# First slab and input in interleaved pieces, constants later, bias rows spread by eight transfers

## The chip, the cores and the metric

The kernel runs on one core of one Trainium2 chip. The metric is the device time of one execution in microseconds (us), as the median over runs; less is better. All numbers are FP32. TensorE multiplies in the FP32R format with every operand split into a high and a low part, so that one product takes three passes.

## The reference

Two blocks of a network run one after the other on 512 tokens of width 1024. The first block has four layers. Each has a mixer (differential attention in layers 0 and 3, HGRN2 in layer 1, sliding-window attention with sinks in layer 2), a layer norm, a squared-ReLU feed-forward of width 4096, a layer norm and a gated per-layer embedding. The second block is one layer with chunkwise retention, an RG-LRU branch and a gated convolutional feed-forward. What bears on the change is the beginning, the differential attention of layer 0 with its relative bias:

```python
def diff_attention(h, w_in, lam, subln, w_out, rel_bias, layer_idx):
    q, k, v = jnp.split(h @ w_in, [DA_QK, 2 * DA_QK], axis=-1)    # 8 heads x 2 maps of 64
    ...
    for blk in range(S // BLOCK):                                   # 4 blocks of 128 queries
        s = jnp.einsum('bmqd,bmkd->bmqk', q[:, :, qs:ke], k[:, :, :ke])
        rel = pos[qs:ke, None] - pos[None, :ke]
        bias = rel_bias[t5_bucket(rel)].transpose(2, 0, 1)          # 16 bias heads
        s = jnp.where(rel >= 0, s + bias, -jnp.inf)
        a = jax.nn.softmax(s, axis=-1).reshape(B, H, 2, BLOCK, ke)
        a = a[:, :, 0] - lam_full * a[:, :, 1]
        outs.append(jnp.einsum('bhqk,bhkv->bhqv', a, v[:, :, :ke]))
```

The bias depends on the distance of query and key alone. Layer 3 uses the same bias; layer 2 uses one of its own with a window of 128.

## The kernel before, in words

**Weights** come as a stream of 287 slabs of 1 MB (128 partitions x 8 x 256), in the order in which `PLAN` lists them. SP issues one DMA a slab into a ring of three (`raw`, L371): the first three at once, slab n when the last unit of slab n - 3 is done (`unit_done`). GpSimd makes the high part of each (`high_part`, `whi`, L393), VectorE the low part (`low_parts`, `wlo`, L1393), which lies in the same bytes as `raw`. VectorE makes it at fixed places of its program, so it waits there for GpSimd, and what is behind it waits too.

**Units.** A unit is eight steps `k` over 1024 input features that fill two PSUM banks with 256 output columns: three matmuls for each of two halves (`feature_chunk`, L410 to L412) or of four token blocks (`token_chunk`, L442 to L444). `begin_unit` waits for the slab's low part (`split_done`) and for the banks of two units before.

**The opening.** ScalarE issues x in four transfers of two feature tiles (L897), then seven constants (L900: `vec`, `ident`, `swapm`, `pick`, `reset`, `tab`, `rb`; all count up the semaphore `loaded`), and makes `gh` from x; VectorE makes `gl` (L1399), with slab 0's `wlo` after the first of the four. TensorE multiplies unit 0; then `start()` multiplies the one-hot table `tab` with `rb` (L489). ScalarE copies the result to DRAM as `bias_table` [16, 1280] (16 heads, 640 values for each of two tables; L908), and when it has landed issues two transfers from DRAM to DRAM which spread the rows: `bias_da` [16, 128, 512] (L910) and `bias_sw` [16, 128, 256] (L911). In them row p of a head is the same line of the table shifted by p:

```python
act.dma_start(bias_da, bass.AP(tensor=table.tensor, offset=127, ap=[[1280, 16], [-1, P], [1, S]])).then_inc(biased, 16)
act.dma_start(bias_sw, bass.AP(tensor=table.tensor, offset=640 + 383, ap=[[1280, 16], [-1, P], [1, 256]])).then_inc(biased, 16)
```

Then ScalarE takes a few small exponentials (L914 to L919), on which a chain of small VectorE operations hangs (L1431 to L1471); behind that chain VectorE makes the low parts of slabs 2, 3 and 4.

**The mixer of layer 0** (`da_mixer`) has four groups of three units (q, k, v for two heads each). ScalarE empties the units into `da_q`, `da_k`, `da_v` (`evac`, L992 to L996). A loop over 32 iterations k (8 heads x 4 query blocks) does `scores(k)` on TensorE (L520), `mask(k)` on VectorE, which adds the bias tile `da_b` (L1591), the exponentials on ScalarE, the transposes (L533) and values (L546) of earlier iterations, and between them nine steps of the next group's units. `scores(k)` waits for `mask(k - 1)`. `bias_in(hd)` on ScalarE (L982) brings the bias of one head pair, 512 KB, from `bias_da` to one of two SBUF buffers; the first two stand between `evac(0, 1)` and `evac(0, 2)` behind a wait for both spreads:

```python
evac(0, 0)
evac(0, 1)
act.wait_ge(biased, 32)
bias_in(0)
bias_in(1)
evac(0, 2)
```

All DMAs that ScalarE issues are on one queue (q10 in the profile), all of SP's on another (q1). Both run on the core's 16 DMA engines.

Of the kernel before, what the change touches and what calls it, by code (L numbers as in the profile page):

```python
# [21 lines left out]
ALU = mybir.AluOpType  # L22
ACT = mybir.ActivationFunctionType

P = 128
S = 512
# [9 lines left out]
HEADS = 8  # L36
# [5 lines left out]
RING = 3  # L42
# [70 lines left out]
PLAN = make_plan()  # L113
N_SLABS = len(PLAN.slabs)
# [65 lines left out]
def build(nc, stream, xin, pin, pos, vecs, relb, onehot, eye, swap, picks, decay, resets, out):  # L180
    with ExitStack() as ctx:
# [11 lines left out]
        raw = place("raw", [P, RING, 8, 256])  # L193
        wlo = place("wlo", [P, RING, 8, 256], F32R, at=raw_at)
# [133 lines left out]
        def sem(name):  # L328
            return ctx.enter_context(nc.semaphore(name))
# [8 lines left out]
        act_own, dve_own = sem("act_own"), sem("dve_own")  # L338
        loaded = sem("loaded")
        x_in = [sem(f"x_in{t}") for t in range(4)]  # L340
        table_out, biased = sem("table_out"), sem("biased")
        m = {}

        def M(name):
            if name not in m:
                m[name] = sem(name)
            return m[name]
# [17 lines left out]
        @block.sync  # L365
        def _(sp):

            for n in range(N_SLABS):
                if n >= RING:
                    sp.wait_ge(unit_done, PLAN.last_unit[n - RING] + 1)  # L370
                sp.dma_start(raw[:, n % RING].rearrange("p k n -> p (k n)"), stream[n]).then_inc(raw_in[n % RING], 16)  # L371

            for t in range(KT):
                sp.wait_ge(M("final_out"), t + 1)
                sp.dma_start(out[:, t, :], fin[:, t, :]).then_inc(M("stored"), 16)
            sp.wait_ge(M("stored"), KT * 16)


        @block.gpsimd
        def _(pool):  # L380
            def low_parts(l, gen):

                for k in range(KT):
                    pool.wait_ge(M("ln_full"), 8 * l + k + 1)

                    pool.wait_ge(*((xh_ready, 4 * gen + k // 2 + 1) if k % 2 else (M("ln_h"), 4 * l + k // 2 + 1)))
                    nc.gpsimd.tensor_tensor(xl[:, k, :], h[:, k, :], xh[:, k, :].bitcast(F32), ALU.subtract)\  # L387
                        .then_inc(xl_ready if k % 2 else M("low_even"), 1)


            def high_part(n):
                pool.wait_ge(raw_in[n % RING], 16 * (n // RING + 1))
                nc.gpsimd.tensor_scalar(whi[:, n % RING], raw[:, n % RING], 1.0, 0.0, ALU.mult, ALU.add).then_inc(hi_done, 1)  # L393

            norm_at = {}
            for layer in range(NL):
                norm_at[PLAN.at[f"ffn{layer}"][0] + 2] = (2 * layer, X_GEN[f"ln1{layer}"])
                norm_at[PLAN.at[f"gate{layer}"][0] + 1] = (2 * layer + 1, X_GEN[f"ln2{layer}"])
            for n in range(N_SLABS):
                if n in norm_at:  # L400
                    low_parts(*norm_at[n])
                high_part(n)
# [3 lines left out]
        def _(pe):  # L406
# [6 lines left out]

            def begin_unit(u):

                pe.wait_ge(split_done, PLAN.unit_slab[u] + 1)
                if u >= 2:
                    e, v = PLAN.released(u - 2)
                    pe.wait_ge(rel[e], v)

            def feature_chunk(u, k, kn, w0, operand):

                slot = PLAN.unit_slab[u] % RING
                oh, ol = operand
                for j in range(2):
                    c = slice(j * P, (j + 1) * P)
                    last = passes(proj[:, 2 * (u % 2) + j, :], (whi[:, slot, w0 + k, c], wlo[:, slot, w0 + k, c]),
                                  (oh[:, k, :], ol[:, k, :]), k == 0, k == kn - 1)
                return last
# [17 lines left out]
            def operand_wait(which, gen, k):  # L447

                if k % 2 == 0:
                    hi, lo = (xh_ready, xl_ready) if which == "x" else (gh_ready, gl_ready)  # L450
                    pe.wait_ge(hi, gen * 4 + k // 2 + 1)
                    pe.wait_ge(lo, gen * 4 + k // 2 + 1)
# [42 lines left out]
            def da_mixer(d, layer):  # L495
# [3 lines left out]
                def chunk(g, c):  # L499
                    u = u0 + 3 * g + c // 8  # L500
                    k = c % 8
                    if k == 0:
                        begin_unit(u)
                    if g == 0 and c < 8:
                        operand_wait("g", gen, k)
                    last = token_chunk(u, k, 8, G) if c // 8 == 2 else feature_chunk(u, k, 8, 0, G)
                    if k == 7:
                        last.then_inc(unit_done, 1)
# [268 lines left out]
            def ret_mixer():  # L777
                s0, u0 = PLAN.at["ret"]
                gen = G_GEN["in4"]
                def chunks(u, first, end):  # L780

                    for c in range(first, end):
                        v, k = u + c // 8, c % 8
                        if k == 0:
                            begin_unit(v)
                        if v == u0:
                            operand_wait("g", gen, k)
                        last = token_chunk(v, k, 8, G) if v - u0 in (2, 3, 8, 9) else feature_chunk(v, k, 8, 0, G)
                        if k == 7:
                            last.then_inc(unit_done, 1)  # L790
# [89 lines left out]
        def _(act):  # L880
# [14 lines left out]
            for t in range(4):  # L895
                p2 = slice(2 * t, 2 * t + 2)
                act.dma_start(h[:, p2, :], xin[:, p2, :]).then_inc(x_in[t], 16)  # L897
            for dst, src in ((vec[:, :], vecs), (ident[:, :], eye), (swapm[:, :], swap), (pick[:, :, :], picks),
                             (reset[:, :], resets), (tab[:, :], onehot), (rb[0:32, :], relb)):
                act.dma_start(dst, src).then_inc(loaded, 16)  # L900
            for t in range(4):
                p2 = slice(2 * t, 2 * t + 2)
                act.wait_ge(x_in[t], 16)
# [3 lines left out]
            mine()  # L907
            act.dma_start(table, tabo[:, :]).then_inc(table_out, 16)  # L908
            act.wait_ge(table_out, 16)
            act.dma_start(bias_da, bass.AP(tensor=table.tensor, offset=127, ap=[[1280, 16], [-1, P], [1, S]])).then_inc(biased, 16)  # L910
            act.dma_start(bias_sw, bass.AP(tensor=table.tensor, offset=640 + 383, ap=[[1280, 16], [-1, P], [1, 256]])).then_inc(biased, 16)  # L911

            act.wait_ge(M("lamsum"), 1)
            A(small[:, 4:8], mix[:, 0, 0:4], ACT.Exp).then_inc(*own.sig(M("lamexp")))  # L914
# [61 lines left out]
            def da_mixer(d, layer):  # L976
                s0, u0 = PLAN.at[f"mix{layer}"]

                def bias_in(hd):
                    if hd >= 2:  # L980
                        act.wait_ge(M("masked"), 64 * d + 8 * (hd - 1))
                    act.dma_start(da_b[:, hd % 2], bias_da[2 * hd:2 * hd + 2].rearrange("m p j -> p m j"))\  # L982
                        .then_inc(M(f"bias_in{hd % 2}"), 16)

# [42 lines left out]
                    A(xh[:, hd, :], post_on[:, :], ACT.Copy, scale=small[:, 10 + d:11 + d]).then_inc(*own.sig(xh_ready if hd % 2 else M("hi_even")))  # L1027

                evac(0, 0)
                evac(0, 1)  # L1030
                act.wait_ge(biased, 32)
                bias_in(0)
                bias_in(1)
                evac(0, 2)
                for k in range(32 + 5):
                    if k < 33 and k % 8 == 0 and 1 <= k // 8 < 4:
                        evac(k // 8, 2)
                    if 1 <= k < 33:
                        second(k - 1)
                    if k < 32:  # L1040
                        exps(k)
                        if k % 4 == 3 and k // 4 + 2 < 8:
                            bias_in(k // 4 + 2)
                    if k < 24 and k % 8 == 3:
                        evac(k // 8 + 1, 0)
                    if k < 24 and k % 8 == 6:
                        evac(k // 8 + 1, 1)
                    if k >= 7 and k % 4 == 3:
                        head_hi((k - 7) // 4)
                    if 2 <= k < 34:  # L1050
                        at_copy(k - 2)
                    if 3 <= k < 35 and (k - 3) % 4 == 3:
                        n = post_base(layer) + (k - 3) // 4
                        head_square(n, M("av"), 32 * d + k - 3 + 1, post_sq)
                        head_std(n, post_rs)
# [72 lines left out]
            def sw_mixer(layer):  # L1128
# [3 lines left out]
                def bias_in(g):  # L1132
                    if g >= 2:
                        act.wait_ge(M("sw_masked"), 16 * (g - 1))
                    act.dma_start(sw_b[:, g % 2], bias_sw[4 * g:4 * g + 4].rearrange("m p j -> p m j")).then_inc(M(f"sw_bias{g % 2}"), 16)

                def evac(g):
# [235 lines left out]
        def _(dve):  # L1373
# [12 lines left out]
            lo_next = [0]  # L1386
# [20 lines left out]
            for t in range(4):  # L1407
                p2 = slice(2 * t, 2 * t + 2)
                low_part(gl[:, p2, :], h[:, p2, :], gh[:, p2, :], gl_ready, gh_ready, t + 1)
                if t == 0:  # L1410
                    low_parts(0)
            low_parts(1)
            dve.wait_ge(loaded, 16 * LOADS)
            mine()
# [225 lines left out]
            def hg_mixer(layer):  # L1640
# [90 lines left out]
                def head_lo(hd):  # L1731
# [2 lines left out]
                    V.tensor_tensor(xl[:, hd, :], hon[:, :], xh[:, hd, :].bitcast(F32), ALU.subtract)\  # L1734
                        .then_inc(*own.sig(xl_ready if hd % 2 else None))

                low_parts(s0 + 2)
                forget(0)
                low_parts(s0 + 3)
# [323 lines left out]
            rms_apply(10, "normf", None, None, None)  # L2063


LOADS = 7


def sw_blocks(n):
# [122 lines left out]
```

## Time and profile before

| | us |
|---|---|
| median of 3 runs (4030.07, 4033.60, 4033.87) | 4033.6 |
| profiled execution | 4028.01 |
| its span | 4026.2 |
| TensorE busy in the span | 3613.0 (90%) |
| VectorE busy | 2040.6 (51%) |
| ScalarE busy | 942.5 (23%) |
| GpSimd busy | 835.2 (21%) |
| mean granted clock of TensorE, share of full speed | 0.952 |

The span is the time between the first and the last instruction of the profiled execution. A busy TensorE isn't TensorE at its peak, since its matmuls are pipelined. The engines other than TensorE are idle for long and for the most part wait for it or for the weights; their idle time costs nothing as long as TensorE has work.

### The profile page before, as it was taken

Reading aid. Unit: us, or ns where it says so; the run is one execution under the profiler, and the core shown is the slowest. Engines: PE = TensorE matmul, PEld = TensorE weight load, DVE = VectorE, ACT = ScalarE, POOL = GpSimd, SP = SyncE. Lnnn points to the kernel's source line nnn. Section 1 sums busy time; section 2 is a strip of 40 time slices with the busy share of each in tenths; the row PEclk is TensorE's granted clock in tenths of the full one; section 3 lists DMA queues with packets and bytes.
Section 4 is the critical chain, followed back from the end, with each engine's and each line's share of the span. In section 5 each row is a group of like instructions: output and inputs, shape, how many; then the busy total and the mean of one; then the engine's idle time right before and its main releaser. Section 6 shows DMA issues by size and latency. Waiting matters only on the chain.

```text
span 4026.2 us, 40463 instructions
## 1 busy us (share of the span) xinstructions
PE 3613.0 (90%) x16680; PEld 2925.9 (73%) x16680; DVE 2040.6 (51%) x2360; ACT 942.5 (23%) x1447; POOL 835.2 (21%) x355
## 2 busy tenths in 40 slices
PE   7987998988779997988998998899968989889998
PEld 6866886777658886756887786688846768778886
DVE  4546335667664336556335554733464335654434
ACT  2542001234321112332001255200121112311101
POOL 1113222200022222103222310322221101222221
PEclk9989999999889998998999999999989989999999
DMA  5212222211012222212222221222211212222322
GB/s 196 84 48 79 94 98 91 75 51 53 32 46 97 103 94 72 88 42 79 94 94 94 84 84 53 79 94 97 103 52 66 74 58 95 86 77 96 103 94 74
DMA packets 55696, 329.50 MB, mean 82 GB/s; under 512 B 5419, under 2 KB 9899, under 8 KB 18652
## 3 DMA queue, kind: packets, MB, share of 16 engines
q1 hardware_dynamic: 42480, 303.06, 21.2%
q10 hardware_dynamic: 13036, 23.85, 1.8%
q8 instruction: 136, 2.23, 0.2%
q14 instruction: 44, 0.36, 0.0%
HBM read 324.45 MB, written 8.47 MB: 83 GB/s over the span
## 4 chain that ended last, share of the span: by engine, by line
PE 79%; DVE 14%; ACT 4%; issue 1%; DMA 1%; POOL 0%; ACTq 0%; DVEq 0%
PE proj L410 23%; PE proj L412 22%; PE proj L411 22%; DVE wlo L1393 3%; DVE tln L1531 2%; DVE h L1533 2%; PE proj L442 1%; PE proj L443 1%; PE proj L444 1%; PE mix L613 1%; PE mix L520 1%; PE mix L546 1%; DVE h L1512 1%; DMA bias_sw<-bias_table 1%; DVE rstd L1524 1%
## 5 line engine op out<-in xcount | busy, mean ns | idle before, releaser
L393 POOL TENSOR_SCALAR whi<-raw 128x2048 fp32r<-128x2048 f32 x287 | 730.1, 2544 | 2914.6 <-DMA raw<-in_stream 2914.6
L410 PE MATMUL proj<-xh,whi 128*128 128x512 f32 x2080 | 834.9, 401 | 177.9 <-POOL xl L387 136.9
L410 PE MATMUL proj<-gh,whi 128*128 128x512 f32 x2184 | 879.8, 403 | 47.1 <-DVE wlo L1393 34.9
L412 PE MATMUL proj<-gh,wlo 128*128 128x512 f32 x2184 | 859.6, 394 | 0.0
L411 PE MATMUL proj<-gl,whi 128*128 128x512 f32 x2184 | 859.2, 393 | 0.0
L411 PE MATMUL proj<-xl,whi 128*128 128x512 f32 x2080 | 823.9, 396 | 0.0
L412 PE MATMUL proj<-xh,wlo 128*128 128x512 f32 x2080 | 823.0, 396 | 0.0
L1393 DVE TENSOR_TENSOR wlo<-raw,whi 128x2048 fp32r<-128x2048 f32 x287 | 681.3, 2378 | 122.3 <-POOL whi L393 103.4
L410 PEld LDWEIGHTS proj<-xh,whi 128*128 128x128 f32 x2080 | 399.8, 192 | 290.4 <-issue 172.9
L410 PEld LDWEIGHTS proj<-gh,whi 128*128 128x128 f32 x2184 | 416.3, 191 | 152.8 <-issue 38.5
L412 PEld LDWEIGHTS proj<-gh,wlo 128*128 128x128 f32 x2184 | 415.3, 190 | 88.9
L411 PEld LDWEIGHTS proj<-gl,whi 128*128 128x128 f32 x2184 | 416.1, 191 | 87.4 <-issue 4.2
L412 PEld LDWEIGHTS proj<-xh,wlo 128*128 128x128 f32 x2080 | 399.2, 192 | 85.4
L411 PEld LDWEIGHTS proj<-xl,whi 128*128 128x128 f32 x2080 | 400.0, 192 | 83.9 <-issue 2.2
L1478 DVE TENSOR_TENSOR h<-h,proj 128x1024 f32<-128x1024 f32 x96 | 117.2, 1221 | 546.2 <-PE proj L412 545.4
L1201 ACT ACTIVATE rl<-proj 128x1024 f32<-128x1024 f32 x64 | 65.6, 1026 | 965.8 <-PE proj L412 965.8
L1836 DVE SCALAR_TENSOR_TENSOR hid<-proj,rl 128x1024 f32<-128x1024 f32 x64 | 78.4, 1225 | 334.5 <-ACT rl L1201 334.1
L442 PE MATMUL proj<-whi,gh 128*128 128x256 f32 (+1 forms) x544 | 161.0, 296 | 3.4 <-DVE wlo L1393 3.4
L443 PE MATMUL proj<-wlo,gh 128*128 128x256 f32 (+1 forms) x544 | 155.3, 285 | 0.0
L444 PE MATMUL proj<-whi,gl 128*128 128x256 f32 (+1 forms) x544 | 155.1, 285 | 0.0
L387 POOL TENSOR_TENSOR xl<-h,xh 128x512 fp32r<-128x512 f32 x64 | 105.2, 1643 | 229.1 <-ACT xh L945 217.5
L926 ACT ACTIVATE sq<-h 128x1024 f32<-128x1024 f32 x40 | 42.5, 1063 | 378.5 <-DVE h L1478 378.5
(288 smaller groups left out, 3240.7 us busy)
## 6 DMA issues: line engine op xcount, KB each, us to landing
raw<-in_stream SPq DMA_DIRECT2D x287, 1024.0 KB, 4.8
da_b<-bias_da ACTq DMA_DIRECT2D x16, 512.0 KB, 3.9
bias_da<-bias_table ACTq DMA_DIRECT2D x1, 4096.0 KB, 22.3
h<-in_x ACTq DMA_DIRECT2D x4, 512.0 KB, 12.1
bias_sw<-bias_table ACTq DMA_DIRECT2D x1, 2048.0 KB, 27.9
pf<-in_p ACTq DMA_DIRECT2D x4, 512.0 KB, 3.4
sw_b<-bias_sw ACTq DMA_DIRECT2D x4, 512.0 KB, 4.1
out_features<-fin SPq DMA_DIRECT2D x8, 256.0 KB, 2.1
```

The source lines that it names most:

```text
L387: nc.gpsimd.tensor_tensor(xl[:, k, :], h[:, k, :], xh[:, k, :].bitcast(F32), ALU.subtract)\
L393: nc.gpsimd.tensor_scalar(whi[:, n % RING], raw[:, n % RING], 1.0, 0.0, ALU.mult, ALU.add).then_inc(hi_done, 1)
L410: nc.tensor.matmul(out, wh, ah, start=first, stop=False, skip_group_check=check)
L411: nc.tensor.matmul(out, wh, al, start=False, stop=False, skip_group_check=check)
L412: return nc.tensor.matmul(out, wl, ah, start=False, stop=last, skip_group_check=check)
L442: nc.tensor.matmul(o, ah, wh, start=k == 0 and st % per == 0, stop=False, skip_group_check=True)
L443: nc.tensor.matmul(o, ah, wl, start=False, stop=False, skip_group_check=True)
L444: last = nc.tensor.matmul(o, al, wh, start=False, stop=k == kn - 1, skip_group_check=True)
L1393: V.tensor_tensor(wlo[:, n % RING], raw[:, n % RING], whi[:, n % RING].bitcast(F32), ALU.subtract).then_inc(*own.sig(split_done))
L1478: V.tensor_tensor(h[:, p2, :], h[:, p2, :], banks(u), ALU.add).then_inc(*own.sig(rel["dve"]))
L1531: V.tensor_tensor(tln[:, k % 2, :], h[:, k, :], rstd[:, :], ALU.mult).then_inc(*own.sig(M("ln_u")))
L1533: V.tensor_scalar(h[:, k, :], tln[:, k % 2, :], col("ln_g", c + k), col("ln_b", c + k), ALU.mult, ALU.add)\
```

## The change

The first slab comes in four pieces of 256 KB on SP's queue, each with a semaphore, while x comes in four on ScalarE's. GpSimd and VectorE split it piece by piece, and in unit 0 TensorE waits for the piece that it needs. SP issues slab 1 when the third part of x has landed, slab 2 when the fourth has. Four constants are issued by SP ahead of slab 2 (`loaded`), the three that are needed from layer 1 on ahead of slab 3 (`loaded_late`). ScalarE runs one small copy before it waits for x.

`bias_da` is spread by eight transfers, one for each head pair with a semaphore of its own; `bias_in(hd)` waits for its own one, and `bias_in(0)` stands ahead of `evac(0, 1)`. `bias_sw` is issued in the mixer loop at k == 18.

```diff
             for n in range(N_SLABS):
...
+            for t in range(4):
+                sp.dma_start(raw[:, 0, 2 * t:2 * t + 2].rearrange("p k n -> p (k n)"), stream[0, :, 512 * t:512 * t + 512]).then_inc(first_in[t], 16)
+            for n in range(1, N_SLABS):
+                if n < RING:
+                    sp.wait_ge(x_in[n + 1], 16)
                 if n >= RING:
                     sp.wait_ge(unit_done, PLAN.last_unit[n - RING] + 1)
+                if n == 2:
+                    for dst, src in (vec[:, :], vecs), (ident[:, :], eye), (tab[:, :], onehot), (rb[0:32, :], relb):
+                        sp.dma_start(dst, src).then_inc(loaded, 16)
+                if n == RING:
+                    for dst, src in (swapm[:, :], swap), (pick[:, :, :], picks), (reset[:, :], resets):
+                        sp.dma_start(dst, src).then_inc(loaded_late, 16)
                 sp.dma_start(raw[:, n % RING].rearrange("p k n -> p (k n)"), stream[n]).then_inc(raw_in[n % RING], 16)
...   # GpSimd
+            for t in range(4):
+                p2 = slice(2 * t, 2 * t + 2)
+                pool.wait_ge(first_in[t], 16)
+                nc.gpsimd.tensor_scalar(whi[:, 0, p2], raw[:, 0, p2], 1.0, 0.0, ALU.mult, ALU.add).then_inc(first_hi if t < 3 else hi_done, 1)
+            for n in range(1, N_SLABS):
...   # TensorE, begin_unit and chunk of da_mixer
-                pe.wait_ge(split_done, PLAN.unit_slab[u] + 1)
+                if u:
+                    pe.wait_ge(split_done, PLAN.unit_slab[u] + 1)
...
+                        if layer == 0 and k % 2 == 0:
+                            pe.wait_ge(*((first_lo, k // 2 + 1) if k < 6 else (split_done, 1)))
...   # ScalarE
-            for dst, src in ((vec[:, :], vecs), (ident[:, :], eye), (swapm[:, :], swap), (pick[:, :, :], picks),
-                             (reset[:, :], resets), (tab[:, :], onehot), (rb[0:32, :], relb)):
-                act.dma_start(dst, src).then_inc(loaded, 16)
+            act.wait_ge(M("start_dve"), 1)
+            A(small[:, 253:254], small[:, 252:253], ACT.Copy).then_inc(*own.sig())
...
-            act.dma_start(bias_da, bass.AP(tensor=table.tensor, offset=127, ap=[[1280, 16], [-1, P], [1, S]])).then_inc(biased, 16)
-            act.dma_start(bias_sw, bass.AP(tensor=table.tensor, offset=640 + 383, ap=[[1280, 16], [-1, P], [1, 256]])).then_inc(biased, 16)
+            for hd in range(HEADS):
+                act.dma_start(bias_da[2 * hd:2 * hd + 2], bass.AP(tensor=table.tensor, offset=127 + 2560 * hd, ap=[[1280, 2], [-1, P], [1, S]]))\
+                    .then_inc(biased[hd], 16)
...   # bias_in of da_mixer; bias_in of sw_mixer waits for biased_sw in the same way
+                    act.wait_ge(biased[hd], 16)
...
                 evac(0, 0)
+                bias_in(0)
                 evac(0, 1)
-                act.wait_ge(biased, 32)
-                bias_in(0)
                 bias_in(1)
                 evac(0, 2)
                 for k in range(32 + 5):
+                    if layer == 0 and k == 18:
+                        act.dma_start(bias_sw, bass.AP(tensor=table.tensor, offset=640 + 383, ap=[[1280, 16], [-1, P], [1, 256]])).then_inc(biased_sw, 16)
...   # VectorE, in the loop over the four parts of x
-                if t == 0:
-                    low_parts(0)
+                low_part(wlo[:, 0, p2], raw[:, 0, p2], whi[:, 0, p2], first_lo if t < 3 else split_done, *((first_hi, t + 1) if t < 3 else (hi_done, 1)))
+            lo_next[0] = 1
...
-LOADS = 7
+LOADS = 4
```

TensorE waits for `loaded_late` at the beginning of the retention mixer and VectorE at the beginning of the HGRN2 mixer. The wait of GpSimd for `raw_in` counts one transfer less in ring place 0.

## Rows read from the trace of the kernel before

**Rows 1.** Waits, 0 to 75 us: who for whom, us in total, times, longest

```profile
PE proj L410 <- DVE wlo L1393: 15.8, 1, 15.8
DVE small L1431 <- ACT small L914: 14.7, 1, 14.7
...
PE proj L442 <- DVE wlo L1393: 3.4, 1, 3.4
...
PE mix L520 <- DVE small L1591: 2.8, 1, 2.8
```

**Rows 2.** Timeline, 35 to 70 us: start, duration, engine, line, operation, idle before

```profile
35.16 0.64 ACTq L910 DMA_DIRECT2D bias_da<-bias_table  x1
35.83 5.17 ACTq L911 DMA_DIRECT2D bias_sw<-bias_table  x1
41.05 0.17 ACT L914 ACTIVATE small<-mix 128x4 f32<-128x4 f32 x1 [7.99 <-issue]
...
45.76 4.49 DVE L1393 TENSOR_TENSOR wlo<-raw,whi 128x2048 fp32r<-128x2048 f32 x2
...
48.10 0.39 PE L442 MATMUL proj<-whi,gh 128*128 128x256 f32 x1 [3.41 <-DVE wlo L1393]
...
61.29 0.49 PE L520 MATMUL mix<-da_k,da_q 64*128 64x128 f32 x4
...
63.79 0.93 ACTq L982 DMA_DIRECT2D da_b<-bias_da  x2
...
68.36 0.29 DVE L1591 CUSTOM_DVE_ANT_0 da_s<-mix,da_b 128x128 f32<-128x128 f32 x1 [8.20 <-DMA da_b<-bias_da]
...
68.92 1.04 PE L520 MATMUL mix<-da_k,da_q 64*128 64x256 f32 x4 [2.84 <-DVE small L1591]
```

**Rows 3.** Windows of 2 us: busy PE, PEld, DVE, ACT, POOL, clock, DMA, GB/s

```profile
49.00:51.00 2.00, 2.00 (x11) 2.00 (x10) 1.25 (x1) 0.00 (x0) 0.00 (x0) 0.50 0.94 302
...
69.00:71.00 2.00, 2.00 (x7) 1.16 (x8) 1.02 (x6) 0.88 (x4) 0.00 (x0) 0.54 0.03 7
```

**Rows 4.** The tile h, 0 to 30 us: durations in ns, min/median/max, then landings

```profile
L904 ACT ACTIVATE gh<-h x4: 1056/1056/1057, 9.5 to 16.6; 128x1024 fp32r<-128x1024 f32 x4
L1399 DVE TENSOR_TENSOR gl<-h,gh x4: 1211/1219/2904, 10.6 to 19.6; 128x1024 fp32r<-128x1024 f32 x4
...
DMA to landing us min/median/max: 7.0/12.1/14.4
```

**Rows 5.** DMA, 35 to 64 us: queue, packets, MB, share; issues, us to landing

```profile
q10 hardware_dynamic: 4128, 6.29, 69.7%
...
bias_da<-bias_table ACTq DMA_DIRECT2D x1, 4096.0 KB, 22.3
bias_sw<-bias_table ACTq DMA_DIRECT2D x1, 2048.0 KB, 27.9
raw<-in_stream SPq DMA_DIRECT2D x2, 1024.0 KB, 8.3
```

**Rows 6.** DMA queues, 0 to 20.3 us: packets, MB, share of 16 engines

```profile
q10 hardware_dynamic: 1388, 3.32, 43.4%
q1 hardware_dynamic: 432, 3.15, 42.2%
```

**Rows 7.** DMA queues, 37 to 40 us

```profile
q10 hardware_dynamic: 478, 0.98, 93.2%
```

**Rows 8.** DMA queues, 64 to 70 us

```profile
q10 hardware_dynamic: 544, 1.05, 46.6%
```

**Rows 9.** DMA queues, 45 to 50 us

```profile
q10 hardware_dynamic: 559, 1.12, 82.0%
```

**Rows 10.** DMA, 35 to 41 us: busy tenths in 40 slices, packets, queues

```profile
DMA  0000000000586499899999998898977699999995
...
DMA packets 666, 1.38 MB, mean 230 GB/s; under 512 B 0, under 2 KB 0, under 8 KB 665
...
q10 hardware_dynamic: 665, 1.36, 68.9%
```

More of the change, by code:

```diff
@@ L340, in build @@
         x_in = [sem(f"x_in{t}") for t in range(4)]
-        table_out, biased = sem("table_out"), sem("biased")
+        loaded_late = sem("loaded_late")
+        first_in = [sem(f"first_in{t}") for t in range(4)]
+        first_hi, first_lo = sem("first_hi"), sem("first_lo")
+        table_out, biased_sw = sem("table_out"), sem("biased_sw")
+        biased = [sem(f"biased{i}") for i in range(HEADS)]
         m = {}
@@ L366, in _ @@
         def _(sp):
-            for n in range(N_SLABS):
+            for t in range(4):
[3 more added lines that the diff above has]
+                    sp.wait_ge(x_in[n + 1], 16)
                 if n >= RING:
                     sp.wait_ge(unit_done, PLAN.last_unit[n - RING] + 1)
+                if n == 2:
[4 more added lines that the diff above has]
+                        sp.dma_start(dst, src).then_inc(loaded_late, 16)
                 sp.dma_start(raw[:, n % RING].rearrange("p k n -> p (k n)"), stream[n]).then_inc(raw_in[n % RING], 16)
@@ L391, in high_part @@
             def high_part(n):
-                pool.wait_ge(raw_in[n % RING], 16 * (n // RING + 1))
+                pool.wait_ge(raw_in[n % RING], 16 * (n // RING + (1 if n % RING else 0)))
                 nc.gpsimd.tensor_scalar(whi[:, n % RING], raw[:, n % RING], 1.0, 0.0, ALU.mult, ALU.add).then_inc(hi_done, 1)
@@ L398, in _ @@
                 norm_at[PLAN.at[f"gate{layer}"][0] + 1] = (2 * layer + 1, X_GEN[f"ln2{layer}"])
-            for n in range(N_SLABS):
+            for t in range(4):
[3 more added lines that the diff above has]
+            for n in range(1, N_SLABS):
                 if n in norm_at:
@@ L779, in ret_mixer @@
                 gen = G_GEN["in4"]
+                pe.wait_ge(loaded_late, 48)
                 def chunks(u, first, end):
@@ L1134, in bias_in @@
                         act.wait_ge(M("sw_masked"), 16 * (g - 1))
+                    act.wait_ge(biased_sw, 16)
                     act.dma_start(sw_b[:, g % 2], bias_sw[4 * g:4 * g + 4].rearrange("m p j -> p m j")).then_inc(M(f"sw_bias{g % 2}"), 16)
@@ L1735, in head_lo @@
                         .then_inc(*own.sig(xl_ready if hd % 2 else None))
+                dve.wait_ge(loaded_late, 48)
                 low_parts(s0 + 2)
```

## The prediction

> **What bounds the kernel now.** I read the page first: TensorE is busy for nine tenths of the span and the chain of waits is almost all its own, so a change to the opening can only move the start of everything behind it, or add a pause. The loops behind the first mixer wait on each other and not on the time of day, so I take a shift of the first mixer over unchanged to the end.
>
> Then the list of waits over the first 75 us [rows 1]. TensorE stands still there several times. It starts at 15.8 us, when VectorE has split the first slab. Between its first and second unit it makes the bias table and waits for ScalarE to read it, which the change leaves as it is. It waits 3.4 us for `wlo` of slab 2, and 2.8 us in front of the second `scores`. The timeline [rows 2] shows why the last two happen. ScalarE issues `bias_da` at 35.16 and `bias_sw` at 35.83; that second issue holds it for 5.17 us, so the small exponentials begin at 41.05. VectorE's chain of small operations hangs on them (it idles 14.7 us), and `wlo` of slabs 2 and 3 stands behind that chain: the first of the pair of 2.25 us is done at 48.0 and TensorE goes on at 48.10. Then ScalarE waits until both spreads are in DRAM, issues `da_b` at 63.79, and `mask(0)` runs at 68.36, `scores(1)` at 68.92. After each of the two pauses the granted clock is at its lower level (0.50 and 0.54 of full speed in the windows of [rows 3]), which costs another 1 to 1.3 us each.
>
> **The start, part by part.** Today the first 512 KB of x land 7.0 us after issue [rows 4], together with the first whole slab: 1.57 MB. After the change x and the slab come in quarters, 0.79 MB for the first pair. The 6.47 MB of [rows 6] took some 18 us, 360 GB/s; the 0.79 MB that are no longer in the first pair are 2.2 us, so the first pair lands near 5.5. Then ScalarE 1.06 us, VectorE 1.22 us for `gl` [rows 4], a quarter of a `wlo` (0.6 us, from the 2.25 of [rows 2]) and 0.15 us of semaphores: TensorE starts at about 8.5 and not at 15.8, a gain of 7.3. The bounds are no saving in the landing (start 10.8) and a landing at 5.0 (start 8.0). Later pairs come every 2.2 us, and TensorE needs over 3 us for a quarter of a unit (13.2 from 48.10 to 61.29 [rows 2]), so it doesn't starve. The constants follow slab 1 on SP's queue and land, by the same 360 GB/s, near 17 us; they are first needed after unit 0, at 8.5 + 13.2 = 21.7. Swap, picks and resets, 0.77 MB or 2 us ahead of slab 3, are hidden: VectorE takes slab 3 only after slab 2. The extra copy on ScalarE loads its table while it waits for x. The late waits cost nothing, their data being older by hundreds of us. `bias_sw` in mid-mixer is one issue of 0.64 us and 6.3 us of queue time (63.8 - 57.5, the two landings by [rows 2, 5]) ahead of a `da_b` that is needed five iterations later; if it held ScalarE for 5.17 us again, it would cost at most those 5 us, once.
>
> **The eight transfers.** This is the part that decides. How many of the 16 DMA engines does a transfer use? ScalarE's queue q10 carried 1388 packets in the opening [rows 6]. Its rows there are 4 x 128 of x, 5 x 128 of constants, 33 of the onehot table and 32 of the rel_bias: 1217. 171 are left. SP's q1 carried 3 x 128 rows and 48 more, that is 16 ending packets a transfer, one for each engine. Ten transfers of 128 or 32 rows on q10 take 160 of the 171; the onehot table with its 33 rows leaves 11. Eleven is the largest number up to 16 that divides 33. The two spreads of today, whose outer dimension is 16 heads, left 32 beside their 4096 rows [rows 5]: 16 each. The new transfers name `[[1280, 2], [-1, P], [1, S]]`, an outer dimension of 2. By the same count each of them runs on 2 engines. The rows don't tell which two; I take the same two each time, because the eight instructions differ in nothing but an offset.
>
> The Trainium skill (DMA: Bandwidth & Descriptors, "Why a DMA increments its semaphore by 16 and not by 1") states this rule: the largest k up to 16 that divides the slowest dimension of both sides. It adds that a transfer issued from SP or ScalarE takes the lowest-numbered k engines. The 11 agrees with the first; which engines are used, no run here shows.
>
> So each of the two engines gets 128 rows of 2 KB a head, 1024 in all, where today it gets 128. What does a row cost? In 37 to 40 us, when all engines did nothing else, 478 of them took 93.2% of 48 engine-us: 94 ns [rows 7]. The cheapest 2 KB rows are those of `da_b`: 544 in 46.6% of 96 engine-us, 82 ns [rows 8]. The dearest stretch is 45 to 50 us: 559 in 82.0% of 80, 117 ns [rows 9]. Two engines ask DRAM for an eighth of what sixteen do, so I take 90, between the cheaper two. 1024 x 0.090 = 92.2 us, and 2.5 us for the two engines' share of slab 4 (8 rows of 8 KB, each four times a 2 KB row at 0.08). With a gain of 7.3 the first is issued at 27.9; rows begin 1.4 us after issue (the first busy slice of [rows 10] is the eleventh of 0.15 us after 35.0, and the issue was at 35.16). The last head is in DRAM at 29.3 + 94.7 = 124.0.
>
> By the skill's table of specifications (same page, about 27 GiB/s an engine) a row would be 71 ns and the eight 72 us; the trace has no 2 KB row that fast.
>
> Two things turn this into a stall.
>
> (a) **ScalarE is held at the issue.** Today the second spread was let go at 41.0, when 665 rows, 42 an engine, had been moved [rows 10], so an instruction passes while about 86 rows an engine of the one before are left. Eighth of eight: 7 x 128 - 86 = 810 rows, 29.3 + 810 x 0.090 + 2.5 = 104.7. Behind it on ScalarE stand the exponentials and `evac(0, 0)`; from there today's rows hold: 41.05 to 48.10 until TensorE has slab 2, then to 66.08 (68.92 less 2.84) until it wants `scores(1)`, 25.0 us. 104.7 + 25.0 = 129.7.
>
> (b) **`da_b` stands behind all eight in the same queue.** A queue keeps its order here: `bias_sw` had been issued at 35.83, but of the 666 packets up to 41.0 none is one of its 1 KB rows [rows 10], and it lands 6.3 us after `bias_da`. So though `biased[0]` comes early, `da_b`'s share on the two engines moves after 124.0, lands near 127 and `scores(1)` follows at 127.6.
>
> The later sets it: 129.7 against 68.92 is 60.8 lost, with everything gained before it. With (a) deciding, there is no pause in front of `scores(1)`, which gives 1 back: 60. If ScalarE isn't held, (b) alone gives 58.7.
>
> **Sum.** Profiled execution: 4028.0 (span 4026.2 and 1.8 around it) + 60 = 4088. The runs shown have their median 5.6 above that execution, so against the median 4033.6 + 60 = **4093 us**. Own bounds: a row at 82 ns makes (a) 123.2, +54, and (b) without (a) 119, +50; at 117 ns (a) gives 151.6, +83. Own range: 4081 to 4117.
>
> **Rivals.**
> 1. *The transfers use all sixteen engines* (faster, the other side). Then the rows cost what they do today: the bias is spread by 27.9 + 22.3 = 50.2, without `bias_sw` behind it, and `da_b` is in 4.6 later, at 54.8, while `scores(1)` is wanted at 38.6 + 18.0 = 56.6. ScalarE is free after eight issues of 0.46 (half of the pair at 63.79 [rows 2]), at 31.6; `wlo` of slab 2 follows 7.0 later, at 38.6, against the end of unit 1 at 37.4 (44.7 - 7.3): of 3.4 us wait 2.2 go. 7.3 + 2.2 + 2.8 + 1.2 for the clock = 13.5, **4020**. For it: the destination of a head is one contiguous run, so its side could be cut in any way. Against: the 11 packets of the table. It decides if a head's transfer ends in 16 packets.
> 2. *Two engines each, but another pair each time, or `da_b` passes the rows ahead of it.* All heads are under way together, head 0 is in at 41, nobody waits: again about **4020**. Against: the order kept in [rows 10], and that (a) alone holds +60 if only `da_b` passes.
> 3. *Dearer rows, or slab loads held up too* (8.3 us for each of two slabs beside the spread [rows 5]; VectorE needs `wlo` of slab 4 ahead of `mask(0)`): at 125 ns a row and 10 us for slabs, +95, **4128**.
> 4. *Little changes*: some of the pairs overlap so that the stall eats just the gain, within 8 us of **4034**; that needs the eight done by 63, 33 us for 4 MB, which is five or six engines. Nothing in the rows gives such a number.
>
> **Chances.** My forecast 0.77, rival 3 0.06, rival 1 0.11, rival 2 0.04, rival 4 0.02. The measurement tells 0.2%, 8 us, from no change. Slower 0.83, faster 0.15, same 0.02. The range takes in the forecast's own range and reaches up over most of rival 3 and a little below, for engines that do better with less beside them: 4074 to 4122. The 0.15 near 4020 is left out.
>
> **What would show it.** TensorE's first matmul near 8.5; ScalarE's issues of `bias_da` with the later ones of about 11 us each and the exponentials near 105; DMA share of about an eighth from 31 to 124; `wlo` of slab 2 near 111; q10 with 16 ending packets for all eight, not 128; after `scores(1)` near 130 the same spacing as today, 60 us later. It is wrong if the share in that stretch is near 0.9, if `bias_da` ends by 50, or if the issues pass at 0.4 us each and `da_b` still lands early.

## The result and the profile after

The changed kernel takes 4087.4 us (median of 4 runs, 4084.9 to 4090.4) against 4031.8 of the kernel before (4 runs, 4025.5 to 4033.9): ratio 1.0135 with a 95% interval of 1.0115 to 1.0155, 55.5 us slower. The forecast was 4093 in a range of 4074 to 4122. Its profiled execution has a span of 4083.1, 56.9 more than before. (The forecast started from 4033.6, the median of three runs of the kernel before; the fourth makes it 4031.8.)

The waits of the changed kernel over its first 140 us, in the form of [rows 1]:

```profile
DVE small L1457 <- ACT small L937: 77.1, 1, 77.1
ACT small L937 <- issue: 74.6, 1, 74.6
...
PE proj L461 <- DVE wlo L1419: 68.5, 1, 68.5
...
PE proj L428 <- DVE wlo L1425: 10.5, 1, 10.5
```

TensorE starts 5.3 us earlier than in [rows 1] and then stands for 68.5 us where it stood for 3.4. The wait in front of the second `scores` is no longer in the list. What it waits for is the chain of [rows 2], link for link, only with other times. The timeline of the changed kernel, ScalarE, then VectorE and TensorE:

```profile
26.76 0.35 ACTq L930 DMA_DIRECT2D bias_table<-tabo  x1
32.41 68.92 ACTq L933 DMA_DIRECT2D bias_da<-bias_table  x8
101.37 0.17 ACT L937 ACTIVATE small<-mix 128x4 f32<-128x4 f32 x1 [74.64 <-issue]
...
101.80 9.67 ACTq L1006 DMA_DIRECT2D da_b<-bias_da  x1
...
106.06 6.69 DVE L1419 TENSOR_TENSOR wlo<-raw,whi 128x2048 fp32r<-128x2048 f32 x3
...
122.55 0.29 DVE L1617 CUSTOM_DVE_ANT_0 da_s<-mix,da_b 128x128 f32<-128x128 f32 x1 [9.80 <-PE mix L541]
...
108.40 0.58 PE L461 MATMUL proj<-whi,gh 128*128 128x256 f32 x1 [68.46 <-DVE wlo L1419]
...
122.01 0.49 PE L541 MATMUL mix<-da_k,da_q 64*128 64x128 f32 x4
...
126.74 0.70 PE L541 MATMUL mix<-da_k,da_q 64*128 64x256 f32 x4
```

The eight issues hold ScalarE for 68.9 us. From its first exponential to TensorE's return are 7.03 us, against 7.05 in [rows 2]. `scores(1)` comes at 126.74 and not at 68.92: 57.8 us later, and the span is 56.9 longer; the 0.9 between them fit the 1 us that the prediction gave back for the clock. Nothing behind the first mixer took part. Two stretches of 3880 us, chosen so that they cover the same work, the changed kernel first (200 to 4080), then the kernel before (143 to 4023):

```profile
200.00:4080.00 3880.00, 3490.75 (x16058) 2829.38 (x16056) 1973.29 (x2196) 893.34 (x1343) 815.18 (x341) 0.95 0.22 79
```

```profile
143.00:4023.00 3880.00, 3493.48 (x16062) 2830.83 (x16060) 1973.13 (x2199) 893.39 (x1343) 815.47 (x341) 0.95 0.22 79
```

The busy times of TensorE's matmuls differ by 3 us in 3880 and those of its weight loads by 1.5; those of the other engines differ by less than 0.3.

**How many engines.** The DMA answers of the changed kernel for 60 to 95 us, when nothing but the spread was under way, and the issue instruction's own line (durations in ns, min/median/max):

```profile
DMA  1111111111111111111111111111111111111111
...
DMA packets 880, 1.79 MB, mean 51 GB/s; under 512 B 6, under 2 KB 6, under 8 KB 880
...
q10 hardware_dynamic: 880, 1.79, 13.1%
```

```profile
L933 ACTq DMA_DIRECT2D bias_da<-bias_table x8: 1216/10136/12347, 32.4 to 91.2; - x8
```

Two of sixteen engines are 12.5%. 874 rows on two engines in 35 us are 80 ns a row, while a packet is recorded with 84 ns (13.1% of 560 engine-us by 874): the rows of an engine overlap a little, so two full engines show as 13.1%. Six packets are smaller than a row, while one instruction passes each 10.1 us: three transfers ended there, with two ending packets each (an ending packet is the small one with which an engine ends its share of a transfer). A transfer has 128 rows an engine, 10.2 us, which is the time between two issues. For most of each 10 us two transfers were queued, and the share and the 51 GB/s never rose, so they all use the same two engines.

From 32.4 us to the end of the last issue, at 101.33, q10 carried this:

```profile
q10 hardware_dynamic: 1605, 3.26, 12.3%
```

12 of the packets are the endings of six transfers. So 797 rows an engine were done, of the 896 ahead of the last transfer: 99 were left when its issue was let go.

**How the two engines hold `da_b`.** The DMA answer from 102 to 121.4 us, the landing of `da_b`; SP's queue moved nothing in this stretch:

```profile
DMA  1111111111111111111119799968641111111111
...
q10 hardware_dynamic: 967, 1.91, 29.4%
```

The first half is the spread on its two engines. `da_b`'s own issue was held for 9.67 us, to 111.5 (ScalarE's next copy, `evac(0, 1)`, waited 8.6 us behind it, with nobody waiting for it). Then the other engines moved their shares of both `da_b` transfers within some 5 us, and the two were again alone at work until 121.4: they had the rest of the spread ahead of their share. That is the prediction's way (b), in the trace.

### The profile page after: what moved, and what is told of

The parts are those of the page before. It is cut to its first block, busy times and chain, and to the rows that moved or that the text cites. A ratio compares the mean times of both kernels' runs of the same rounds, so it can differ in the third digit from the quotient of the medians.

```text
span 4083.1 us, 40495 instructions
## 1 busy us (share of the span) xinstructions
PE 3610.3 (88%) x16680; PEld 2924.9 (72%) x16680; DVE 2039.7 (50%) x2363; ACT 943.0 (23%) x1448; POOL 838.6 (21%) x358
## 4 chain that ended last, share of the span: by engine, by line
PE 79%; DVE 13%; ACT 4%; ACTq 2%; issue 1%; POOL 0%; DMA 0%; DVEq 0%
PE proj L428 23%; PE proj L429 22%; PE proj L430 22%; DVE wlo L1419 2%; ACTq L933 2%; DVE tln L1557 2%; DVE h L1559 2%; PE proj L461 1%; PE proj L462 1%; PE proj L463 1%; PE mix L634 1%; PE mix L541 1%; PE mix L567 1%; DVE h L1538 1%; DVE rstd L1550 1%
## 5 line engine op out<-in xcount | busy, mean ns | idle before, releaser
L461 PE MATMUL proj<-whi,gh 128*128 128x256 f32 (+1 forms) x544 | 161.5, 297 | 68.5 <-DVE wlo L1419 68.5
L461 PEld LDWEIGHTS proj<-whi,gh 128*128 128x128 f32 x544 | 106.0, 195 | 75.7 <-DVE wlo L1419 68.9
```

The costliest lines, as they stand in the source:

```text
L461: nc.tensor.matmul(o, ah, wh, start=k == 0 and st % per == 0, stop=False, skip_group_check=True)
```

## The experiments

Each was timed in turns with the kernel before on the same chip; ratios are to it, with 95% intervals. Its median was 4032.3 us beside experiments 1 to 4 and 4030.0 beside 5 to 8.

**1. Eight transfers of another shape.** In the changed kernel each transfer takes 16 rows of all 16 maps.

```diff
-act.dma_start(bias_da[2 * hd:2 * hd + 2], bass.AP(..., offset=127 + 2560 * hd, ap=[[1280, 2], [-1, P], [1, S]]))
+act.dma_start(bias_da[:, 16 * hd:16 * hd + 16], bass.AP(..., offset=127 - 16 * hd, ap=[[1280, 16], [-1, 16], [1, S]]))
...   # bias_in
-act.wait_ge(biased[hd], 16)
+for i in range(HEADS if hd == 0 else 0):
+    act.wait_ge(biased[i], 16)
```

> The changed kernel, but each of the eight transfers of bias_da takes 16 rows of all 16 maps (outer dimension 16) and not all rows of 2 maps; bias_in(0) waits for all eight. Same number of transfers, rows and bytes. Two-engine theory: each transfer runs on 16 engines and leaves 16 ending packets, the last issue passes near 36.5 us (86 rows an engine may be outstanding), TensorE has slab 2 at 43.5, scores(1) at 61.5 without a pause: 8 us faster than the kernel before, 64 faster than the changed one. Rival 'eight transfers and their semaphores cost, not their shape': the issues stay near 10 us each and the time near 4087. Rival 'the new opening delays the table and the slabs': some of the 55 us stay.

Measured: 4027.5 us, ratio 0.9988 (0.9977 to 0.9998), 5 us faster than before, which the interval just tells from no change. Its DMA queue from 33 to 53.9 us, its issues and its wait for slab 2:

```profile
q10 hardware_dynamic: 2178, 4.20, 64.1%
```

```profile
L933 ACTq DMA_DIRECT2D bias_da<-bias_table x8: 624/645/1192, 33.9 to 39.0; - x8
```

```profile
PE proj L461 <- DVE wlo L1420: 6.7, 1, 6.7
```

2178 packets are the 2048 rows, 128 endings (eight times 16) and 2 more. The issues pass at 0.65 us and not at 10.1. The same number of transfers, rows and bytes is some 60 us cheaper, so neither the number of transfers nor their semaphores cost anything like the loss; what is left is the shape. Slab 2's low part was 3.8 us later than expected (47.3 and not 43.5): the table was in at 33.9, 1.5 later; ScalarE was free at 40.2, its hold being 6.3 us; and some 7 us for the small chain followed. That is why 5 us were gained and not 8.

**2. The opening alone**, with the two old transfers and their order in `da_mixer`.

> The kernel before with the new opening alone (pieces, gates, constants on SP); the bias is spread by the two old transfers, waited for together. Two-engine theory: TensorE starts at 10.5 as in the changed kernel, bias_da is issued at 32.4, the small exponentials run at 38.3, slab 2's low part is there at 45.3 (48.1 before), da_b lands near 65.7, scores(1) at 66.1 (68.9 before): 3 us faster than the kernel before. Rival 'the opening is what costs': slower than before by tens of us.

Measured: 4027.2 us, ratio 0.9991 (0.9982 to 1.0000). TensorE starts at 10.7, has slab 2 at 43.2 and `scores(1)` at 64.0. The opening isn't what costs; it gives 5 us here, at the edge of what the measurement tells. `bias_da` was issued at 31.4 and took 21.4 us, both a little less than expected.

**3. The bias part alone**, in the kernel before.

> The kernel before with the bias part of the change alone (eight transfers of 2 maps, their waits, the second table at k == 18); the opening is the old one. Two-engine theory: bias_da is issued at 35.2, ScalarE is held 69 us, goes on at 104, scores(1) near 129: 59 us slower than the kernel before, 4091. Rival 'the opening is what costs': no slower than before, perhaps 3 us faster.

Measured: 4088.2 us, ratio 1.0140 (1.0124 to 1.0156), 56 us slower. Its waits:

```profile
PE proj L443 <- DVE wlo L1398: 67.0, 1, 67.0
PE proj L411 <- DVE wlo L1398: 15.7, 1, 15.7
```

The whole loss is in this part. The median of the changed kernel is within 1 us of it. In the profiled executions `scores(1)` comes at 130.6 here and at 126.7 in the changed kernel, 3.8 us apart, 2.9 of which are the earlier begin of the eight transfers (32.4 against 35.3). So of the 5.3 us by which TensorE starts earlier some 1 to 4 are left behind the stall; with four runs of each kernel, 5 to 7 us apart among themselves, the medians don't tell how much.

**4. Four transfers of four maps.**

```diff
-for hd in range(HEADS):
-    act.dma_start(bias_da[2 * hd:2 * hd + 2], bass.AP(..., ap=[[1280, 2], [-1, P], [1, S]])).then_inc(biased[hd], 16)
+for hd in range(0, HEADS, 2):
+    act.dma_start(bias_da[2 * hd:2 * hd + 4], bass.AP(..., ap=[[1280, 4], [-1, P], [1, S]])).then_inc(biased[hd], 16)
...   # bias_in
-act.wait_ge(biased[hd], 16)
+act.wait_ge(biased[hd - hd % 2], 16)
```

> The changed kernel with four transfers of 4 maps in place of eight of 2; the same bytes and rows. Two-engine theory, extended: an outer dimension of 4 means 4 engines, 4 + 1 ending marks a transfer, DMA share 0.25 and 102 GB/s. A transfer is 128 rows an engine as before; the last of four passes after 3 x 128 - 86 = 298 rows, at 33.9 + 298 x 0.0795 + 3 = 60.6; slab 2 at 67.6, scores(1) at 85.6: 16 us slower than the kernel before, 4048. Rival 'a fixed hold of some 10 us for each transfer': ScalarE would be held for about 30 us less than with eight of them all the same, but the DMA rate would stay at 51 GB/s, the bias would be complete near 120 and scores(1) near 123.

Measured: 4050.1 us, ratio 1.0043 (1.0030 to 1.0055), 18 us slower. Its timeline on ScalarE, and its DMA from 50 to 61 us:

```profile
32.33 28.89 ACTq L933 DMA_DIRECT2D bias_da<-bias_table  x4
61.26 0.17 ACT L937 ACTIVATE small<-mix 128x4 f32<-128x4 f32 x1 [33.62 <-issue]
```

```profile
DMA packets 552, 1.12 MB, mean 102 GB/s; under 512 B 4, under 2 KB 4, under 8 KB 552
...
q10 hardware_dynamic: 552, 1.12, 26.2%
```

Four engines, 102 GB/s, four ending packets for the one transfer that ended there (the expectation has one more); `scores(1)` comes at 87.1 and not at 85.6. ScalarE is free at 61.3 where 60.6 was worked out. A fixed hold for each transfer is ruled out: the transfers still took 128 rows an engine, but the bytes went twice as fast. From 32.4 us to the end of the fourth issue, at 61.22, q10 has this:

```profile
q10 hardware_dynamic: 1167, 2.37, 21.8%
```

Without 8 ending packets these are 290 rows an engine of 384, so 94 were left. Outer dimensions of 2, 4 and 16 gave 2, 4 and 16 engines.

**5. The exponentials ahead of the eight issues**, in the changed kernel. It asks what is left of the stall when a part of ScalarE's hold no longer counts.

```diff
 act.dma_start(table, tabo[:, :]).then_inc(table_out, 16)
+act.wait_ge(M("lamsum"), 1)
+...   # the four small activations, moved up unchanged
 act.wait_ge(table_out, 16)
 for hd in range(HEADS):
```

> The changed kernel with ScalarE's small exponentials ahead of its wait for the table and the eight issues of 2 maps. It tells apart the two ways in which the slow transfers stall: (a) through ScalarE, held at the issue, (b) through da_b, which stands behind them in the queue. If only what hangs on the exponentials mattered, TensorE would go on with slab 2 at about 40 and the time fall by over 60. By (a) as a whole evac(0, 0) still stands behind the issues, so TensorE waits for its banks until 102.4, 6 us earlier than the 108.4 of the changed kernel; by (b) da_b lands at 121.4 all the same, so scores(1) comes at 122, and of the 6 us some 4 to 5 are left: 4083.

Measured: 4087.6 us, ratio 1.0139 (1.0125 to 1.0153), no change against the changed kernel, where 4 to 5 us less were expected. TensorE's and VectorE's waits, and `da_b` to its landing:

```profile
PE proj L461 <- ACT da_q L1016: 62.7, 1, 62.7
...
PE mix L541 <- DVE small L1617: 3.9, 1, 3.9
```

```profile
DVE da_s L1617 <- DMA da_b<-bias_da: 72.1, 1, 72.1
```

```profile
DMA to landing us min/median/max: 13.7/18.1/22.5
```

TensorE goes on at 103.1, 5.3 us earlier, and `scores(0)` comes at 116.4, 5.6 earlier; but then `mask(0)` waits for `da_b`, issued at 101.9 and in 22.5 later, at 124.4, and `scores(1)` comes at 125.1, 1.6 us earlier than in the changed kernel. Even that is lost: the granted clock fell while TensorE waited, as the windows of 126 to 128 us show, the changed kernel first, then this one:

```profile
126.00:128.00 2.00, 2.00 (x11) 1.19 (x10) 0.51 (x3) 0.00 (x0) 0.85 (x1) 1.00 0.12 49
```

```profile
126.00:128.00 2.00, 2.00 (x6) 1.45 (x5) 1.32 (x7) 0.51 (x4) 0.00 (x0) 0.50 0.02 4
```

The clock is at its lower level, half the upper one, and `scores(2)` comes at 132.7 against 131.7, so that nothing is left of the gain.

In the changed kernel `da_b` landed 19.6 after 101.80, at 121.4, so way (b) alone, with `scores(1)` following 0.6 us later, gives 122.0: 53 us of the 57.8. Way (a), through ScalarE, gives the 126.74 that was measured and lay 4.7 us behind it. That (b) takes over as soon as (a) is some us shorter is what this run shows; that it would hold nearly the whole loss if ScalarE weren't held at all is worked out from these times and was not run, since `evac(0, 0)` still stands behind the eight issues here (TensorE waits 62.7 us for it).

Of the 3 us by which `da_b` was later here, 0.8 are a later begin of the spread. The rest fits a weight slab that crossed `da_b`: from 102 us to its landing SP's queue moved nothing in the changed kernel, and here it moved this:

```profile
q1 hardware_dynamic: 144, 1.05, 13.3%
```

TensorE went on earlier and so asked for the next slab before `da_b` was in; eight rows of 8 KB on each of the two engines are, at four times 80 ns, 2.6 us. This is an estimate.

**6. By rows, and the exponentials first.** Experiments 1 and 5 together.

> The kernel with eight transfers of 16 rows of all maps, and ScalarE's small exponentials ahead of its wait for the table. The 6.7 us that TensorE waits for slab 2's low part at 47.3 go, with the fall of its clock (1.3 us); da_b lands near 58 as before, so scores(1) comes at 58.7 and not at 66.1. Theory: 7 us off that kernel, 4020, 12 less than the kernel before. Rival 'the pause only moves to da_b': scores(1) near 63 and 4024.

Measured: 4018.4 us, ratio 0.9969 (0.9956 to 0.9981), 12 us faster than before. `scores(1)` at 60.9 and not at 66.1; of the 6.7 us wait for slab 2 there are 2.3 left, in which TensorE waits for `evac(0, 0)` behind the issues. Two more waits keep it from the 58.7 expected: 1.8 us in front of `scores(0)` for `evac(0, 1)`, which stands behind `bias_in(0)` and so behind the wait for all eight transfers, and 0.6 in front of `scores(1)`.

**7. The late constants later**: swap, picks and resets ahead of slab 6.

```diff
-if n == RING:
+if n == RING + 3:
     for dst, src in (swapm[:, :], swap), (pick[:, :, :], picks), (reset[:, :], resets):
```

> As the one with the exponentials first, and swap, picks and resets are issued ahead of slab 6 and not of slab 3. Theory: the bias table took 5.6 us to land in the changed kernel and 2.0 in the kernel before because SP's 0.77 MB of constants and slab 3 were under way; without the constants it lands some 2 us earlier, the bias too, and what is left of the wait for da_b goes: 1 to 2 us off. Rival 'slab 3 alone fills the engines': no difference.

Measured: 4013.3 us, ratio 0.9958 (0.9946 to 0.9970), 17 us faster than before and 74 faster than the changed kernel (4087.4, and 4087.6 for experiment 5, which was timed beside it). The DMA answers from 26 to 33 us, the changed kernel first, then this one:

```profile
q1 hardware_dynamic: 341, 1.44, 57.0%
...
bias_table<-tabo ACTq DMA_DIRECT2D x1, 80.0 KB, 5.6
```

```profile
q1 hardware_dynamic: 88, 0.59, 20.0%
...
bias_table<-tabo ACTq DMA_DIRECT2D x1, 80.0 KB, 2.1
```

The 80 KB of the table land in 2.1 us again. That was worth 5 us and not the 1 to 2 expected: the spread begins at 28.8 and not at 33.3, `evac(0, 0)` is no longer late, and TensorE's only wait left in front of `scores` is one of 0.4 us; `scores(1)` comes at 56.5.

**8. Slab 0 whole**, rows of 8 KB, otherwise as experiment 6.

> As the one with the exponentials first, but slab 0 comes in one transfer with rows of 8 KB; x in four pieces, slabs 1 and 2 gated as before. In the changed kernel the first x piece landed at 7.0 us and not at the 5.5 forecast; the DMA rate was 170 to 210 GB/s from 2 to 6 us. Theory 'rows of 2 KB are what is slow at the start': the first x piece lands earlier than 7.0 or as the slab does, near 6.5, and TensorE starts at or before 10.5. Rival 'the first rows are slow whatever their size': the same rate at first, the slab is in near 8.5 and TensorE starts near 11.5.

Measured: 4021.8 us, ratio 0.9973 (0.9962 to 0.9984), 3 us slower than experiment 6, though the two intervals overlap. Windows from 2 to 6 us, the changed kernel first, then this one (the last three columns are clock, DMA share, GB/s):

```profile
2.00:4.00 2.00, 0.00 (x0) 0.00 (x0) 0.00 (x0) 0.74 (x1) 0.00 (x0) 1.00 0.88 169
4.00:6.00 2.00, 0.00 (x0) 0.00 (x0) 0.00 (x0) 0.75 (x2) 0.00 (x0) 1.00 0.82 214
```

```profile
2.00:4.00 2.00, 0.00 (x0) 0.00 (x0) 0.00 (x0) 1.27 (x1) 0.00 (x0) 1.00 0.88 246
4.00:6.00 2.00, 0.00 (x0) 0.00 (x0) 0.00 (x0) 0.21 (x2) 0.00 (x0) 1.00 1.01 387
```

Both sides were half right. The short rows seem to be a good part of what makes the first us slow: 246 and 387 GB/s against 169 and 214, and the kernel before, with whole slabs too, has 262 and 356 in the same windows. But there are also fewer and larger transfers in both, which no run takes apart. And whole rows bring 1 MB where a quarter is wanted: x's first piece is used at 7.8 and not at 7.1, and TensorE starts at 11.7 and not at 10.6. The pieces are worth 1.1 us of start, of which `scores(1)` keeps 0.7 (60.9 against 61.7).

## Why the prediction was right

The mechanism and the side were right, the sizes near. That the total is as near as 3 us is partly luck: the spread began 4.5 us later than forecast, and ScalarE's hold was 8 us shorter. By its steps:

- **Two engines a transfer.** Shown, by share (13.1%), ending packets (two each) and by the series 2, 4, 16. The count of 11 ending packets for the 33-row table [rows 6] was enough to find it. That they are the same two each time was a choice; the share that stays at two sixteenths shows it. It agrees with what the Trainium skill says in DMA: Bandwidth & Descriptors, "Why a DMA increments its semaphore by 16 and not by 1", that a transfer issued from ScalarE takes the lowest-numbered k engines; which two they are, no run here shows. Rivals 1 and 2 fall with it, rival 3 since rows got cheaper and not dearer, and rival 4 by the 55.5 us.
- **The price of a row.** Forecast 90 ns, measured 80 between rows, or 84 in busy time, which is how the prediction's 82, 94 and 117 were made: two engines alone run about as fast as the cheapest rows seen before, the 82 ns of [rows 8]. That alone makes the hold 8 us shorter (810 rows).
- **The start.** Forecast 8.5, measured 10.5. The step that was mis-sized is the landing: quarter pieces were given the DMA rate of the whole opening, 360 GB/s, and got 169 to 214 at first; x's first piece landed after 6.3 us and not 4.8. Experiment 8 suggests short rows as a part of it.
- **The constants ahead of slab 3.** Called hidden, and wrong. I looked at who waits for slab 3 and not at what else was in the engines. The bias table was issued 6.3 us earlier than before (26.76 against 33.09: 5.3 from the start, 1.1 from a shorter unit 0), but took 5.6 us to land and not 2.0, so 2.8 were left at the first spread (32.4 against 35.2). In this kernel that cost some 3 us under a stall of 57; without the stall, experiment 7 shows 5 us.
- **(a) ScalarE held.** Forecast free at 104.7, measured 101.4: the spread began 4.5 us later (2.0 from the start, 3.6 from the table's landing, less 1.1 from unit 0), the rows cost 8 less. The count of 86 outstanding rows an engine was a little low. It was 99 in the changed kernel and 94 in experiment 4; at 80 ns the difference is 1 us, so the forecasts of the hold came out (in experiment 4, 60.6 forecast and 61.3 measured).
- **From there 25.0 us to `scores(1)`.** Measured 25.4.
- **(b) `da_b` in the queue.** Forecast a landing at 127 and `scores(1)` at 127.6, 2.1 us ahead of the 129.7 of (a). Measured 121.4, which allows 122.0, 4.7 ahead of the 126.7 of (a). The cheaper rows take 10 us off (b) and 8 off (a). Experiment 5 takes 5.3 us off (a), and the time stays.
- **`bias_sw` in mid-mixer.** Its issue took 0.60 us. Experiments 1, 6 and 7 have it and are faster than before; what it costs by itself wasn't tried.
- **The own range.** Its upper end is the worked one (+83). Its lower end, 4081, is 2 to 3 us under the +50 that was worked out for it; nothing hung on that.

The sum: 60 forecast, 57 in the profiled executions, 55.5 between the medians.

## What to carry to other kernels

A transfer that is cut smaller is not cheaper per byte if the cut makes its outermost dimension small: write down that dimension for each new transfer and count the engines it leaves, here 2 of 16 for two maps and 16 for sixteen rows of all maps. A queue that is slow stalls twice, its issuing engine and each later transfer behind it, so look at both before hoping that an early piece will be early. And when transfers are moved to where nobody waits for them, look for a small transfer with a waiter that they will now share the engines with.

## What the runs showed of the hardware beyond that

- An issue is held until a part of the rows of the instruction before it has gone. 86 rows an engine were left on 16 engines [rows 10], 94 to 102 for most issues on 2 and 4 engines in the changed kernel and experiments 3 to 5, and 121 to 124 for one issue of each of them. It took 5.17 us for one spread behind another on 16 engines [rows 2], 10.1 us for most of them on 2, and 28.9 us in all for four on 4. `da_b`, which puts only 16 rows on each of 16 engines, was held behind them for 9.67 us all the same.
- With 2 or 4 engines at work each copies 2 KB rows from DRAM to DRAM in 80 ns, 25.6 GB/s (84 ns by busy time); by busy time all sixteen together took 94 to 117 ns [rows 7, 9].
- In the first us of the kernel, 2 KB and 4 KB rows gave 169 to 214 GB/s at 82 to 88% busy engines, and some 400 from 6 us on. Why they are slow only at first, no run tells.
